# Convolution, silu and splits of the mLSTM branch moved from the heads into the input projection

## The chip, the core and the metric

The kernel runs on one core of a Trainium2 chip. The metric is the device time of one execution in microseconds (us); lower is better. The kernel before takes 4286.54 us (median of three executions, 4284.75 to 4287.95). Engines are named as the profile does: PE (matmuls), PEld (its weight loads), DVE, ACT, POOL, SP. Each has a queue of its own, and they meet at semaphores.

## The reference, cut to what matters

One transformer-like block on 512 tokens of width 2048: a norm, an input projection, an S5 branch with a gated linear unit (GLU), an mLSTM branch, a merge, an output projection, and a PEER layer with 16384 experts. The part that the change touches is the front of the mLSTM branch:

```python
def causal_conv(x, w, b):
    seq = x.shape[1]
    xp = jnp.pad(x, ((0, 0), (CONV_WIDTH - 1, 0), (0, 0)))
    out = b
    for j in range(CONV_WIDTH):
        out = out + xp[:, j:j + seq] * w[j]
    return out
...
    xc = jax.nn.silu(causal_conv(xm, conv_w, conv_b))
    q = jnp.einsum('bshd,hde->bshe', heads(xc), w_q).astype(f32)
    k = (jnp.einsum('bshd,hde->bshe', heads(xc), w_k) * MLSTM_HEAD_DIM ** -0.5).astype(f32)
    v = jnp.einsum('bshd,hde->bshe', heads(xm), w_v).astype(f32)
...
    h = h * mh_gain.astype(f32) + skip.astype(f32) * xc.astype(f32)
```

xm is 1536 channels wide: four heads of 384 channels, each three blocks of 128. q, k and the skip use xc, v uses xm itself.

## The kernel before

**Arithmetic.** Every matmul on weights is done three times on fp32r halves: an operand is split into a high part (a copy that ACT writes, `whi`, `xc_hi`) and a low part (operand minus high part, `wlo`, `xc_lo`, on DVE or POOL), and `mm3` (L1730) runs high x high, high x low, low x high. Activations lie transposed, 128 channels on the partitions and 512 tokens along a row.

**Weights.** All weights come as a stream of units of 128x2048 (1 MB). SP loads a unit into one of two `raw` buffers when its last content has been split (L301 to L306). ACT makes `whi` (L653), DVE `wlo` (L1038), each one unit ahead of PE. In the input projection one unit gives one output block of 128 channels: 16 x 3 matmuls, 10.9 us.

**Input projection.** Blocks 0 to 3 are the S5 input, 4 to 15 xm (U_XM to U_Z), 16 to 27 z, 28 to 59 the merge gates. For each xm block ACT splits the next unit (L690), waits for PE, copies the result from PSUM to `stage[:, k, :]` (L693) and stores it to the DRAM tensor `spill` (L695). Two stage buffers take turns. DVE only makes the low parts of the units (L1204 to L1206). Behind the xm blocks DVE prepares the gates of the mLSTM: two additions (L1211, L1212) and one operation (L1213), whose semaphore `ge_sem` releases ACT's exponential (L702); after it ACT goes on with the z blocks, their first unit split first. POOL is idle in this stage; its first work afterwards is the store of the gates (L370).

**S5 and GLU.** During blocks 28 to 59 the S5 recurrence runs beside the projection. Then come eight GLU units of four output chunks each (PE from L1811): PE makes value and gate chunks into two pairs of banks, ACT takes the sigmoid of a gate chunk (L756), DVE multiplies (L1322, waits for the store of ya two products earlier), POOL multiplies with `sa`, stores `ya_d` (L435) and reloads `sa` (L440). Before this loop POOL loads xmr, the three xm blocks of head 0, from `spill` (L416), and DVE, ACT and POOL make the convolution, silu and split of head 0: `conv(step, 0, c)`, `conv_high(0, c)`, `conv_lo(0, c)`.

**Heads.** Four heads, one after another, in an order written out by hand for each engine. PE in `head` (L1839): six q and k blocks from xc (nine matmuls each), the mean of the previous head's output (L1829, waits for POOL's multiplication with z) after the third, its squares (L1836, wait for ACT's L768, that for DVE's L1330) after the fifth, then scores and values, den (L1877) and the weighted sum. Banks are few: a block's bank is free when DVE has made its low part (L1364, L1366), and scores(0) waits for all six. Into this order the convolution of the *next* head is woven: DVE `conv` (L1294, one L1300 and three L1302 per block, on xmr), ACT `conv_high` (silu into `xcf` L736, copy to `xc_hi` L739) and POOL `conv_lo` (L422), between the blocks q1, q2 and k4 or k5. `xmr` is reloaded for the next head in `next_xm` (L472), which waits until the convolution and the low parts of xm have read it. POOL's `skips` (L459) add `xc_hi` and `xc_lo` back together for the skip term.

## Time and profile before

| | us |
|---|---|
| median of three executions | 4286.54 |
| the profiled execution, its own time | 4285.1 |
| its span from first to last instruction | 4283.6 |
| busy: PE, DVE, ACT, POOL | 4065.0, 2508.7, 1226.7, 1129.3 |
| xm and part of the z blocks of the projection | 107 to 334 |
| GLU | 827 to 927 |
| heads and their tail | 927 to 1195 |
| everything behind (merge, output projection, PEER) | 1195 to 4283.6 |

A row of a timeline gives the start, the duration, the engine, the line, the operation, and in brackets how long the engine was idle before and what released it. A row of windows gives a stretch, its length, the busy time of each engine in it with its instructions, the granted clock of PE as a share of full speed (1.00 is 2.4 GHz, 0.50 is 1.2 GHz), the busy share of the DMA engines and GB/s. A matmul of 512 columns is shown as 0.39 us long, and one starts every 0.227 us at full clock.

### The profile page before, as it was taken

The page shows a single profiled execution, that of the slowest core. Times are in us where ns is not written, and L with a number is a line of the kernel's source. Part 1 is how long each engine was busy: PE and PEld are TensorE (multiplying, and loading weights), DVE is VectorE, ACT ScalarE, POOL GpSimd, SP SyncE. Part 2 cuts the span into 40 slices and gives each one's busy share as a digit, 9 for nine tenths or more (in the row PEclk, how much of TensorE's full clock was granted, in tenths as well). Part 3 has the DMA queues.
Part 4 walks back from the last instruction along what each step waited for, and adds up shares of the span by engine and source line. Part 5 has one row for each costly group of instructions (what it writes and reads, how often), then busy time and mean ns, then how long its engine had stood idle before and what let it go on. Part 6 is the DMA issues. An engine that isn't in the chain of part 4 may idle for free.

```text
span 4283.6 us, 54780 instructions
## 1 busy us (share of the span) xinstructions
PE 4065.0 (95%) x19189; PEld 3474.4 (81%) x19189; DVE 2508.7 (59%) x3563; ACT 1226.7 (29%) x1282; POOL 1129.3 (26%) x742
## 2 busy tenths in 40 slices
PE   7999999887789989999999999999989999999997
PEld 4887666665677768888888888888879999999996
DVE  5226888837653254454566666222237888788874
ACT  3232222234322222222233333222222222232222
POOL 1002334433211144545300000000012444444432
PEclk9999999998899989999999999999999999999998
DMA  3332222342154344554677777866767888888883
GB/s 120 120 115 98 98 100 96 108 152 79 51 175 142 127 135 162 173 170 161 209 238 239 255 241 238 295 216 215 222 232 262 302 306 325 308 327 304 307 315 114
DMA packets 225639, 840.57 MB, mean 196 GB/s; under 512 B 21720, under 2 KB 60136, under 8 KB 157600
## 3 DMA queue, kind: packets, MB, share of 16 engines
q1 hardware_dynamic: 96432, 454.07, 29.3%
q10 hardware_dynamic: 95808, 207.64, 15.6%
q0 software_dynamic: 33328, 178.08, 11.5%
q8 instruction: 25, 0.41, 0.0%
q14 instruction: 46, 0.38, 0.0%
HBM read 753.70 MB, written 220.23 MB: 227 GB/s over the span
## 4 chain that ended last, share of the span: by engine, by line
PE 72%; DVE 13%; issue 6%; DMA 4%; ACT 3%; POOL 2%; DVEq 1%; ACTq 0%; SPq 0%; POOLq 0%
PE mm L1732 18%; PE mm L1733 18%; PE mm L1734 17%; DMA raw<-stream 3%; PE pv L1732 3%; PE pv L1733 3%; PE pv L1734 3%; DVE wlo L1038 2%; PE sc L1734 1%; PE sc L1733 1%; PE sc L1732 1%; DVE acc L1658 1%; ACT whi L653 1%; DVE tab L1258 1%; POOL el L611 1%
## 5 line engine op out<-in xcount | busy, mean ns | idle before, releaser
L1038 DVE TENSOR_TENSOR wlo<-raw,whi 128x2048 fp32r<-128x2048 f32 x328 | 753.4, 2297 | 882.4 <-ACT whi L653 881.9
L653 ACT ACTIVATE whi<-raw 128x2048 fp32r<-128x2048 f32 x380 | 727.4, 1914 | 499.6 <-issue 198.7
L1732 PE MATMUL mm<-t_hi,whi 128*128 128x512 f32 x2048 | 798.5, 390 | 0.0
L1733 PE MATMUL mm<-t_lo,whi 128*128 128x512 f32 x2048 | 797.8, 390 | 0.0
L1734 PE MATMUL mm<-t_hi,wlo 128*128 128x512 f32 x2048 | 797.3, 389 | 0.0
L1734 PEld LDWEIGHTS mm<-t_hi,wlo 128*128 128x128 f32 x2048 | 384.6, 188 | 80.4
L1732 PEld LDWEIGHTS mm<-t_hi,whi 128*128 128x128 f32 x2048 | 384.8, 188 | 78.1
L1733 PEld LDWEIGHTS mm<-t_lo,whi 128*128 128x128 f32 x2048 | 384.8, 188 | 77.7
L1732 PE MATMUL mm<-hn_hi,whi 128*128 128x512 f32 x960 | 380.6, 396 | 34.3 <-DVE hn_lo L1074 19.3
L1733 PE MATMUL mm<-hn_lo,whi 128*128 128x512 f32 x960 | 376.6, 392 | 0.0
L1734 PE MATMUL mm<-hn_hi,wlo 128*128 128x512 f32 x960 | 375.9, 392 | 0.0
L617 POOL DMA_INDIRECT gv<-ev_d,idx_v x128 | 230.1, 1798 | 513.7 <-DVE acc L1658 468.7
L550 POOL TENSOR_TENSOR wlo<-raw,whi 128x2048 fp32r<-128x2048 f32 x52 | 239.3, 4603 | 301.0 <-ACT whi L653 301.0
L1658 DVE SCALAR_TENSOR_TENSOR acc<-gv,ac,acc 128x2048 f32<-128x2048 f32 x127 | 298.2, 2348 | 32.5 <-DMA gv<-ev_d,idx_v 30.3
L894 ACT ACTIVATE sgl<-mm 128x512 f32<-128x512 f32 x128 | 76.7, 599 | 744.9 <-PE mm L1734 744.8
L1732 PEld LDWEIGHTS mm<-hn_hi,whi 128*128 128x128 f32 x960 | 181.7, 189 | 95.6 <-issue 33.8
L611 POOL DMA_INDIRECT el<-up_d,idx_e x128 | 198.2, 1548 | 88.0 <-DVE ac L1664 49.2
L1734 PEld LDWEIGHTS mm<-hn_hi,wlo 128*128 128x128 f32 x960 | 181.9, 189 | 38.5
L1733 PEld LDWEIGHTS mm<-hn_lo,whi 128*128 128x128 f32 x960 | 182.0, 190 | 36.5
L961 ACT ACTIVATE actb<-gl 128x384 f32 (+1 forms) x128 | 67.3, 526 | 492.5 <-DVE gl L1633 484.6
L1732 PE MATMUL pv<-actb,whi 128*128 (+1 forms) x512 | 173.0, 338 | 13.7 <-DVE wlo L1038 13.7
L1732 PE MATMUL mm<-actb,whi 128*128 (+1 forms) x512 | 171.7, 335 | 0.4 <-DVE wlo L1038 0.3
(395 smaller groups left out, 7553.1 us busy)
## 6 DMA issues: line engine op xcount, KB each, us to landing
raw<-stream SPq DMA_DIRECT2D x380, 1024.0 KB, 4.9
ev_d<-stream ACTq DMA_DIRECT2D x128, 1024.0 KB, 6.1
up_d<-sgl ACTq DMA_DIRECT2D x128, 256.0 KB, 2.1
g_d<-gst ACTq DMA_DIRECT2D x12, 2048.0 KB, 11.5
gg<-g_d SPq DMA_DIRECT2D x15, 1536.0 KB, 12.0
gl<-up_d SPq DMA_DIRECT2D x120, 192.0 KB, 5.0
spill<-stage ACTq DMA_DIRECT2D x56, 256.0 KB, 2.0
x<-xT SPq DMA_DIRECT2D x4, 1024.0 KB, 9.4
```

The source lines that it names most:

```text
L550: pool.tensor_tensor(wlo[:, nk, :], raw[:, nk, :], whi[:, nk, :].bitcast(F32), ALU.subtract)\
L611: pool.indirect_dma_start(el[:, s:s + 1], None, ups_flat, bass.IndirectOffsetOnAxis(ap=idx_e[:, s:s + 1], axis=0)).then_inc(el_in, 16)
L617: pool.indirect_dma_start(gv[s % 3][:], None, ev_d, bass.IndirectOffsetOnAxis(ap=idx_v[:, 0, s:s + 1], axis=0))\
L653: act.activation(whi[:, k, :], raw[:, k, :], ACT.Copy).then_inc(hi_done, 1)
L894: act.activation(sgl[:, k, :], mm[k][:], ACT.Gelu_apprx_tanh).then_inc(proj_free, 1)
L961: act.activation(actb[:, par, 0, v, :], gl[:, v % 2, :], ACT.Copy).then_inc(acthi_done, 1)
L1038: dve.tensor_tensor(wlo[:, k, :], raw[:, k, :], whi[:, k, :].bitcast(F32), ALU.subtract)\
L1258: ins = dve.scalar_tensor_tensor(ts_[:, w:2 * w], tc_[:, 0:w], psin, dtmp[:, 1, 0:w], ALU.mult, ALU.add)
L1658: dve.scalar_tensor_tensor(acc[:], gv[b][:], ac_cols[:, s, :], acc[:], ALU.mult, ALU.add)\
L1732: pe.matmul(out, lh, rh, start=start, stop=False)
L1733: pe.matmul(out, lh, rl, start=False, stop=False)
L1734: return pe.matmul(out, ll, rh, start=False, stop=stop)
```

## The change

The convolution, the silu and the split into high and low part are done for each of the twelve xm blocks during the input projection. DVE convolves from `stage` into `cv` as soon as ACT has copied the block there. ACT takes the silu in place and makes the high part into `xcs`, one block later in its order: split of the next unit, silu and high part of the block before, copy of the block itself. DVE makes the low part in the following block, after the weights' low part. POOL stores both parts to a new DRAM tensor `xc_d`, 512 KB a block. Before the GLU loop POOL loads them all into `xc_hi` and `xc_lo` with four transfers on its queue (two of 768 KB for head 0, two of 2304 KB for heads 1 to 3), placed behind the loads of xmr and sa. PE waits for them before head 0 and before head 1. The heads no longer hold `conv`, `conv_high`, `conv_lo` and the waits that belonged to them. xmr is still loaded per head, for v. A buffer of its own, `nt_h`, serves the Newton step of `scale`.

```diff
+            with pool.Fori(0, MC // 2) as p:
+                for k in range(2):
+                    pool.wait_ge(xclo_done, 2 * p + k + 1)
+                    pool.dma_start(xc_d[2 * p + k].rearrange("r p t -> p r t"), xcs[:, k, :, :]).then_inc(xc_out[k], 16)
...
-            for c in range(HC):
-                conv_lo(0, c)
-
+            for k in range(2):
+                pool.wait_ge(xc_out[k], 16 * (MC // 2))
+            xc_src = xc_d.rearrange("c r p t -> r p c t")
+            for g, cs in enumerate((slice(0, HC), slice(HC, MC))):
+                for r, dst in enumerate((xc_hi, xc_lo)):
+
+                    pool.wait_ge(proj_done, O_GLU)
+                    pool.dma_start(dst[:, cs, :], xc_src[r, :, cs, :]).then_inc(xc_in[g], 16)
...
-                pool.wait_ge(cv_done, 3 * h + 3)
                 pool.wait_ge(xmlo_done, 3 * h + 3)
                 pool.dma_start(xmr[:], xm_heads[h + 1]).then_inc(xm_in, 16)
...
-                if not last:
-                    for c in range(HC):
-                        conv_lo(h + 1, c)
                 if not first:
-
-                    pool.wait_ge(xclo_done, 3 * h + (3 if last else 6))
                     skips(h - 1, (0, 1))
...
+            def conv_high(n, k):
+
+                act.wait_ge(cv_done, n + 1)
+                act.activation(cv[:, k, :], cv[:, k, :], ACT.Silu).then_inc(silu_done, 1)
+                met()
+                act.wait_ge(silu_done, n + 1)
+                act.wait_ge(xc_out[k], 16 * (n // 2))
+                act.activation(xcs[:, k, 0, :], cv[:, k, :], ACT.Copy).then_inc(xchi_done, 1)
+
+            def mlstm_tile(m, k, first=False):
+                n = 2 * (m - U_XM // 2) + k
+                next_hi(m, k, (proj_done, 2 * m + k))
+                if not first:
+                    conv_high(n - 1, 1 - k)
+                act.wait_ge(proj_done, 2 * m + k + 1)
+                act.wait_ge(stage_out[k], 16 * (m - U_XM // 2))
+                act.activation(stage[:, k, :], mm[k][:], ACT.Copy).then_inc(proj_free, 1)
+                act.wait_ge(proj_free, 2 * m + k + 1)
+                act.dma_start(spill[2 * m + k - U_XM], stage[:, k, :]).then_inc(stage_out[k], 16)
+
+            mlstm_tile(U_XM // 2, 0, first=True)
+            mlstm_tile(U_XM // 2, 1)
+            with act.Fori(U_XM // 2 + 1, U_Z // 2) as m:
+                for k in range(2):
+                    mlstm_tile(m, k)
+            conv_high(MC - 1, 1)
...
-            for c in range(HC):
-                conv_high(0, c)
-
...
                 qkv(0)
                 qkv(1)
-                if not last:
-
-                    if not first:
-                        act.wait_ge(hf_done, 3 * (h - 1))
-                    act.wait_ge(xclo_done, 3 * h + 3)
-                    conv_high(h + 1, 0)
                 qkv(2)
-                if not last:
-                    conv_high(h + 1, 1)
                 if not first:
                     tail_squares(h - 1)
                 qkv(3)
                 qkv(4)
                 qkv(5)
-                if not last:
-                    conv_high(h + 1, 2)
...
+            def conv(n, k):
+
+
+                one, count = stepper(ml_step, 3 * n)
+                o, i = cv[:, k, :], stage[:, k, :]
+                tap = [cols(V_CW + MC * j, MC)[:, n, :] for j in range(4)]
+                dve.wait_ge(proj_free, U_XM + n + 1)
...
+            next_lo(U_XM // 2, 0)
+            conv(0, 0)
+            next_lo(U_XM // 2, 1)
+            conv_lo(0, 0)
+            conv(1, 1)
+            with dve.Fori(U_XM // 2 + 1, U_Z // 2) as m:
                 for k in range(2):
                     next_lo(m, k)
+                    conv_lo(2 * m + k - U_XM - 1, 1 - k)
+                    conv(2 * m + k - U_XM, k)
+            conv_lo(MC - 1, 1)
...
-            dve.wait_ge(xm_in, 16)
-            for c in range(HC):
-                conv(step, 0, c)
-
...
-                dve.wait_ge(silu_done, MC if last else 3 * h + 6)
-                newton(one, rs[:], rd[:], cv[:, 1, :])
+                newton(one, rs[:], rd[:], nt_h[:])
...
-                pe.wait_ge(xclo_done, 3 * h + 3)
...
             pe.wait_ge(onesr_done, 1)
+            pe.wait_ge(xc_in[0], 32)
             head(0, True)
+            pe.wait_ge(xc_in[1], 32)
             with pe.Fori(1, HEADS) as h:
```

## Rows read from the trace of the kernel before

**Rows 1.** Windows: projection, GLU, heads; start:end, length, busy time of PE, PEld, DVE, ACT, POOL

```profile
107.00:334.00 227.00, 227.00 (x1003) 188.00 (x1003) 54.98 (x33) 62.73 (x51) 0.00 (x0) 1.00 0.34 120
827.00:927.00 100.00, 92.80 (x388) 75.90 (x389) 40.75 (x37) 35.93 (x37) 41.36 (x48) 0.93 0.49 172
927.00:1195.00 268.00, 188.14 (x798) 147.59 (x796) 172.87 (x245) 101.67 (x157) 79.82 (x72) 0.85 0.22 70
```

**Rows 2.** Waits of PE from 820 to 1200: total us, times, longest us

```profile
PE st L1829 <- POOL hh L452: 20.3, 3, 9.6
```

**Rows 3.** Timeline of PE in the GLU and the heads, rows behind a gap

```profile
846.35 0.80 PE L1732 MATMUL mm<-y_hi,whi 128*128 128x512 f32 x1 [4.85 <-DVE vt L1322]
...
956.13 0.79 PE L1732 MATMUL sc<-q_hi,k_hi 128*128 128x512 f32 x1 [17.42 <-DVE k_lo L1366]
...
998.96 3.78 PE L1836 MATMUL dn<-ex,ones 128*128 128x512 f32 x4 [5.03 <-ACT ex L768]
...
1016.11 0.39 PE L1732 MATMUL sc<-q_hi,k_hi 128*128 128x256 f32 x1 [1.34 <-DVE pf L1383]
...
1060.55 2.46 PE L1836 MATMUL dn<-ex,ones 128*128 128x512 f32 x4 [3.89 <-ACT ex L768]
...
1118.37 1.88 PE L1836 MATMUL dn<-ex,ones 128*128 128x512 f32 x4
...
1124.58 0.50 PE L1732 MATMUL sc<-q_hi,k_hi 128*128 128x512 f32 x1 [1.41 <-DVE k_lo L1366]
```

**Rows 4.** Windows, for the granted clock behind the busy times (third from the end)

```profile
848.00:853.00 5.00, 5.00 (x18) 3.99 (x18) 2.01 (x1) 0.00 (x0) 3.74 (x5) 0.77 0.59 192
...
942.00:959.00 17.00, 2.87 (x7) 2.30 (x8) 9.61 (x16) 9.12 (x14) 3.80 (x3) 0.51 0.11 46
...
997.00:1004.00 7.00, 5.04 (x7) 2.19 (x7) 4.95 (x8) 3.74 (x7) 1.27 (x1) 0.51 0.00 1
...
1062.00:1065.00 3.00, 3.00 (x6) 1.35 (x5) 2.65 (x5) 0.50 (x2) 0.00 (x0) 0.50 0.00 0
```

**Rows 5.** Timelines of ACT before the first sigmoid, of DVE in head 0

```profile
842.86 0.63 ACT L739 ACTIVATE xc_hi<-xcf 128x512 fp32r<-128x512 f32 x1
...
939.83 0.55 DVE L1300 TENSOR_SCALAR cv<-xmr,vec 128x512 f32<-128x512 f32 x1 [7.92 <-DMA xmr<-spill]
...
955.39 0.68 DVE L1366 SCALAR_TENSOR_TENSOR k_lo<-mm,k_hi 128x512 fp32r<-128x512 f32 x1
```

**Rows 6.** Timelines: one block's convolution, silu and split; a unit's low part

```profile
944.10 0.63 ACT L736 ACTIVATE xcf<-cv 128x512 f32<-128x512 f32 x1
944.82 0.63 ACT L739 ACTIVATE xc_hi<-xcf 128x512 fp32r<-128x512 f32 x1
...
993.70 0.54 DVE L1300 TENSOR_SCALAR cv<-xmr,vec 128x512 f32<-128x512 f32 x1
994.38 2.54 DVE L1302 SCALAR_TENSOR_TENSOR cv<-xmr,vec,cv 128x511 f32<-128x511 f32 x3
...
240.94 2.29 DVE L1038 TENSOR_TENSOR wlo<-raw,whi 128x2048 fp32r<-128x2048 f32 x1 [8.22 <-ACT whi L653]
```

**Rows 7.** Timeline of ACT between the xm blocks and the z blocks

```profile
235.77 0.60 ACT L693 ACTIVATE stage<-mm 128x512 f32<-128x512 f32 x1 [7.51 <-PE mm L1734]
...
237.70 1.28 ACT L653 ACT_TABLE_LOAD   x1
238.99 1.92 ACT L653 ACTIVATE whi<-raw 128x2048 fp32r<-128x2048 f32 x1
246.72 1.28 ACT L693 ACT_TABLE_LOAD   x1 [5.81 <-PE mm L1734]
```

**Rows 8.** DMA issues (KB each, median us to landing); landings of xres, min/median/max

```profile
h<-h_d POOLq DMA_DIRECT2D x1, 4096.0 KB, 15.1
...
key_raw<-keys POOLq DMA_DIRECT2D x1, 1024.0 KB, 7.2
...
DMA to landing us min/median/max: 2.8/3.0/9.6
```

More of the change, by code:

```diff
@@ L456, in skips @@
                 for c in blocks:
-                    if c >= 2:
-                        pool.wait_ge(hf_done, 3 * h + c - 1)
+                    pool.wait_ge(hf_done, 3 * h + c - 1 if c >= 2 else 3 * h)
                     pool.tensor_tensor(xcf[:, c % 2, :], xc_hi[:, 3 * h + c, :].bitcast(F32),
@@ L1291, in _ @@
                 assert count[0] == S5_STEPS, count
-            def conv(one, h, c):
-                dve.wait_ge(silu_done, 3 * h + 1 if c == 2 else 3 * h)
-                o, i = cv[:, c % 2, :], xmr[:, c, :]
-                tap = [cols(V_CW + MC * j, MC)[:, 3 * h + c, :] for j in range(4)]
-                one(dve.tensor_scalar(o, i, tap[3], cols(V_CB, MC)[:, 3 * h + c, :], ALU.mult, ALU.add))
-                for lag in (1, 2, 3):
-                    ins = dve.scalar_tensor_tensor(o[:, lag:T], i[:, 0:T - lag], tap[3 - lag], o[:, lag:T],
-                                                   ALU.mult, ALU.add)
-                    if lag < 3:
-                        one(ins)
-                    else:
-                        ins.then_inc(cv_done, 1)
             split_lo(U_GLU // 2, 1)
-            dve.wait_ge(xm_in, 16)
-            for c in range(HC):
-                conv(step, 0, c)
             with dve.Fori(0, 4) as q:
@@ L1392, in head @@
                 qkv(1)
-                if not last:
-                    dve.wait_ge(xm_in, 16 * h + 32)
-                    conv(one, h + 1, 0)
                 qkv(2)
-                if not last:
-                    conv(one, h + 1, 1)
                 if not first:
@@ L1402, in head @@
                 qkv(4)
-                if not last:
-                    conv(one, h + 1, 2)
                 if not first:
@@ L1443, in _ @@
                 dve.wait_ge(ya_out[b], 16 * 8)
-            one, count = stepper(ml_step, 0)
+            one, count = stepper(ml_step, 3 * MC)
             head(one, 0, True, False)
```

40 lines of the change are left out of this document (21 added, 19 removed).

## The prediction

> **What bounds the kernel now.** I read the busy shares of each stage first, then what PE waits for, then the timelines of PE, DVE and ACT at those waits. In the stretch in which the input projection makes the mLSTM blocks PE is busy 227.00 of 227 us, while DVE has 55 and ACT 63 [rows 1]: whatever DVE and ACT do there beside it is free as long as every next weight block is split before PE asks for it. In the gated linear unit (GLU) PE has 92.8 of 100 us. In the four heads and their tail it has 188 of 268 us: 80 us without a matmul, the only place here with something to win. The reader is to see in [rows 3] which waits make them up. Before the scores of head 0 PE is idle for 17.42 us, before the squares (L1836) 5.03 us in head 1 and 3.89 in head 2, before the third score block 1.34 us, and inside the GLU 4.85 us. The longest waits besides, 20.3 us in three pieces, stand before the mean over the channels [rows 2]; a reciprocal and the finish of the previous head lead there, and no convolution. The clock follows the gaps: it stands at 0.51 of full, that is at its lower level of 1.2 GHz, from 942 to 959 and from 997 to 1004, at 0.50 from 1062 to 1065, and at 0.77 in the five microseconds behind the GLU's gap [rows 4].
>
> **Which of these waits are the convolution's.** Head 0: PE has all six q and k blocks by 938.7 (17.42 before 956.13). But DVE starts its next convolution only when the reload of xmr has landed (939.83, 7.92 us idle), and its last k_lo, which releases the scores, starts at 955.39, behind three convolutions that alternate with ACT's silu [rows 5]. Heads 1 and 2: ACT stands at silu and its split ahead of the squares. Head 3 has no convolution and is the template: its squares start without a wait, the first four take 1.88 us where they took 3.78 in head 1 and 2.46 in head 2, it has no wait before its third score block, and it keeps only the 1.41 us between the last k block and the scores [rows 3]. GLU: ACT is in the third split of head 0 until 843.5, so the first sigmoids are late [rows 5].
>
> **Heads, part by part.** Removed from DVE per block: 0.54 + 2.54 us; from ACT 0.63 + 0.63; from POOL one subtraction [rows 6]. None of that sum is the gain; the gaps are.
> Head 0: 17.42 becomes 1.41, that is 16.0. What is late next is the load of the gate rows, which follows xmr on POOL's queue; it delays the first exponents by some 3 us, but PE has two score and two value blocks (about 6.8 us) before it needs them, so I take nothing for it. The scores also ran at half clock from 956.13 to about 959.5, 3.4 us for 1.7 us of work [rows 3, 4]. Together 17.7.
> Head 1: 5.03 and 1.34 go. From the start of the squares at 998.96 until about 1004 PE works at half clock, 5.0 us for 2.5 us of work [rows 4], so 2.5 more. Together 8.9.
> Head 2: 3.89, the same 1.34, and three microseconds at half clock (1062 to 1065) for 1.5 of work. Together 6.7.
> The waits before the mean stay: their chain starts at the last value block of PE itself, and is the same in all heads. The xm reload loses a wait on the convolution and is issued no later. POOL's two skip additions now stand directly behind the gate loads, as in head 3.
> Heads: 33.3 us gained.
>
> **GLU.** The 4.85 us go, and with them some 2 us that the following matmuls lost at low clock (0.77 over five us, [rows 4]); 6.8. Against it: 6 MB (24 blocks of 256 KB) of loads are put on POOL's queue ahead of the reload of sa and of the stores of ya, and DVE's third product waits for the first of these stores. How the queue treats this a row shows: the reloads of xres land in 3.0 us in the median, but in up to 9.6 us where they stand behind the 1 MB of key_raw, which itself took 7.2; so the later ones wait for the earlier. The 4 MB of h came in 15.1 us beside other traffic [rows 8], so 6 MB take about 22.6; issued from about 828 on, they end near 851. PE needs the third product at about 852 (two units of four chunks, 48 matmuls at 0.227 us each, behind 841.5). So it is level to within a microsecond. I take 1 us of stall; bounds 0 (queue not in order) and 8 (loads a third slower, or behind a weight load, with the clock lost again). GLU: 5.8 gained, bounds 6.8 gained and 1 lost.
> The Trainium skill, page "DMA: Bandwidth & Descriptors", section "Queues, rings and completion order", says the same of order (descriptors are consumed in ring order, rows take turns), and its section "Bandwidth" puts the HBM side at about 358 GB/s for a core: by that figure alone an estimate for the 6 MB is 17.6 us, the stall would be nothing and the time 1 us lower.
>
> **Input projection.** Added per block, twelve times: convolution 3.2, low part 0.69 on DVE; silu and high part 1.35 on ACT; a 512 KB store on POOL's queue, where nothing else stands until the gates. DVE then has 2.29 + 3.2 + 0.7 = 6.2 us and ACT 1.92 + 0.60 + 1.35 = 3.9 of the 10.9 us that a block takes PE [rows 6, 7]. The order within a block: stage at 0.2 to 0.8, convolution until 4.0, low part of the next weights until 6.3, and PE wants it at 10.9. The cover is 4.6 us. Here, 0, until the stage ends.
> At its end the cover is missing. The last mLSTM block is copied at 235.77. Until now ACT went on with the gates' exponential at once, loaded a table (1.28) and had the next weights split at 240.9, DVE by 243.2; PE asks for them at about 246.5, when it leaves the block between [rows 7]. After the change ACT's exponential waits for DVE's three gate operations, which stand behind the last convolution and its low part, and that one waits for ACT. The chain: 236.4, convolution 3.0, silu and split 1.4, low part 0.75, three gate operations at about 0.75 each (a third of the 2.54 that three of 511 columns take is 0.85, [rows 6]), exponential 0.65, table 1.3, high part 1.95, low part 2.3: 250.0. PE waits 3.5 us (at 3.2 for the convolution 3.7). A second table load on the chain (silu and exp) would make it 4.8, and a gap of this size cost clock above; I put 5 us, bounds 2 and 8.
> The trace shows one load as 1.28 us with the next activation right behind it (237.70 + 1.28 = 238.98) [rows 7]. The Trainium skill, page "ScalarE: Activation LUTs", section "What ACT_TABLE_LOAD costs", adds a drain of 1.38 us to each; this row shows none. By the page the seam would cost 1.4 us more for each load on its chain.
>
> **The sum.** The profiled execution took 4285.1 us (span 4283.6), 1.4 below the median of 4286.54. Heads -33.3, GLU -5.8, seam +5: -34.1. 4251.0 for that execution, 4252.4 for a median: 4252.
>
> **The rivals.**
> A, forecast: about 4252, within 8 us (bounds of seam and GLU, and clock windows that fall differently). 0.60.
> B, queue: the loads of xc on POOL's queue end at 860 or later, PE stands 8 us in the GLU and starts again at half clock. For it: the order shown in [rows 8], and 2 KB pieces where h had long ones. Against it: the rate above. 4252 + 8 to 10 = 4261. 0.14.
> C, only head 0: the gaps in heads 1 and 2 change owner, since DVE or the mean's chain is late there anyway. For it: DVE is busy 173 of 268 us in this stretch [rows 1]. Against it: head 3. Gain without 15.5: 4268. 0.09.
> D, better: no stall in GLU, seam 2 us, less time at low clock in the heads: 4244 or lower. 0.09.
> E, slower: the projection's cover fails. Per block DVE's low part now stands behind the convolution, that behind ACT's stage, and ACT's silu behind both. If this circle takes longer than PE's 10.9 us, each of twelve blocks pays the excess. It stands at 6.3, so it decides from 4.6 us more per block than worked out, and the whole is slower by over 0.2% from 3.6 us beyond that (43 us over twelve blocks eat the 34). What could add as much is a table load before each of a block's four activations: at 1.28 us they make 11.4 us, an excess of 0.5, 6 us in all, 4258; at double that price 16.5 us, an excess of 5.6, 67 us in all, 4319. Against it: the one load in [rows 7] is followed at once by its activation, ACT is idle 7.51 us before a stage, and DVE is busy a quarter of this stretch. 0.04.
> The double price is near that of the Trainium skill, page "ScalarE: Activation LUTs", section "What ACT_TABLE_LOAD costs": about 2.66 us for a switch; its section on table sets lists copy among the functions of every set, and by that E can't come about.
> F, the edit moves little: the heads' waits turn out to be others' and the seam and the queue cost what B and their upper bounds say; within 8.6 us of now. 0.04.
>
> **Chances and range.** 0.2% is 8.6 us, about what a measurement of this kernel can tell from no change. Faster: A to D nearly whole, 0.91; same: F and a corner of C, 0.05; slower: E, 0.04. The range reaches from the better half of D to B and the near edge of C: 4240 to 4267.
>
> **What would show it.** PE in the projection without a gap up to about 246, then one gap of 3 to 5 us behind which ACT's whi ends near 248. In the GLU no gap at the third unit, or one that a late landing of ya ends. Head 0: one gap of 1.4 before its scores in place of 17.4, and first scores near 940 on the old clock. Heads 1 and 2: no gap before the squares, none before the third score block; the gaps of 9.6 and 8.0 before the mean still there. What would make me wrong: a gap in every projection block (E), a GLU gap over 5 us (B), or squares that still wait (C).

## The result and the profile after

The changed kernel takes 4250.6 us (median of 4 runs, 4247.31 to 4252.15) against 4286.13 us for the kernel before on the same chip (4 runs, 4284.75 to 4287.95). The ratio is 0.9917, with a 95% interval of 0.9904 to 0.9930. Run a second time, in a longer comparison, it took 4251.5 us, ratio 0.9926 (0.9912 to 0.9939). The forecast was 4252.

The page of the profiled execution of the changed kernel, which took 4247.31 us itself: its span, the engines, the queue that GpSimd issues on (packets, MB, share of 16 DMA engines), and the shares of the chain that ended last.

```profile
span 4245.8 us, 54861 instructions
...
PE 4051.5 (95%) x19189; PEld 3466.7 (82%) x19189; DVE 2514.0 (59%) x3575; ACT 1226.3 (29%) x1280; POOL 1132.2 (27%) x746
...
q0 software_dynamic: 39728, 190.67, 12.5%
...
PE 76%; DVE 10%; issue 5%; DMA 3%; POOL 2%; ACT 2%; DVEq 0%; ACTq 0%; SPq 0%; POOLq 0%
```

The busy time of no engine fell by anything like 35 us; PE's 13.5 us less are the same 19189 matmuls, of which fewer run at the lower clock. DVE and ACT do the same work as before, at another place. What fell is waiting: PE's share of the chain rose from 72 to 76%, DVE's fell from 13 to 10.

Windows of the changed kernel that answer to [rows 1]; each stage starts elsewhere now, so the second and third are set to its start. Columns: start:end, length, busy time of PE, PEld, DVE, ACT and POOL, granted clock, DMA share, GB/s.

```profile
107.00:334.00 227.00, 223.31 (x979) 184.41 (x978) 93.51 (x97) 80.10 (x76) 8.70 (x12) 0.99 0.42 143
...
836.00:928.00 92.00, 90.44 (x385) 74.20 (x386) 30.56 (x24) 30.10 (x29) 39.80 (x48) 0.97 0.74 252
...
927.00:1195.00 268.00, 212.35 (x935) 169.78 (x936) 166.92 (x226) 99.31 (x144) 73.50 (x71) 0.90 0.29 94
```

The projection: DVE went from 55 to 93.5 us and ACT from 63 to 80, and PE lost 3.7 us, at one place. The GLU is whole in 92 us, where it needed 98.4, though its DMA share went from 0.49 to 0.74. In the same 268 us behind it PE is busy 212 us instead of 188 and its clock is 0.90 instead of 0.85.

The timeline of PE after, rows at the places of [rows 3]. Columns: start, duration, engine, line, operation, and in brackets the idle time before it and who ended it.

```profile
251.33 0.65 PE L1738 MATMUL mm<-hn_hi,whi 128*128 128x512 f32 x1 [3.69 <-DVE wlo L1043]
...
835.84 0.79 PE L1738 MATMUL mm<-y_hi,whi 128*128 128x512 f32 x1 [3.52 <-DVE y_lo L1323]
...
927.74 0.47 PE L1738 MATMUL mm<-xc_hi,whi 128*128 128x512 f32 x1 [1.56 <-DVE vt L1337]
...
941.65 0.50 PE L1738 MATMUL sc<-q_hi,k_hi 128*128 128x512 f32 x1 [1.41 <-DVE k_lo L1379]
...
977.74 1.88 PE L1842 MATMUL dn<-ex,ones 128*128 128x512 f32 x4
...
1022.55 1.22 PE L1835 MATMUL st<-hh,ones 128*128 128x512 f32 x1 [9.62 <-POOL hh L462]
...
1076.04 1.22 PE L1835 MATMUL st<-hh,ones 128*128 128x512 f32 x1 [8.15 <-POOL hh L462]
...
1282.22 0.70 PE L1738 MATMUL mm<-mg_hi,whi 128*128 128x512 f32 x1 [3.42 <-DVE mg_lo L1474]
```

Between 835.84 and 927.74 no row of PE has a wait in brackets: the GLU's gap is gone. Head 0 has 1.41 us before its scores for 17.42. The four squares of head 1 (977.74) have no wait and take 1.88 us, the value of head 3 before. The waits of 9.6 and 8.2 us before the means (1022.55, 1076.04) stand as they stood. New is the first row, 3.69 us where the projection goes over from the mLSTM blocks to the z blocks.

The two fixed points by which I measure the heads with their tail are the first q matmul and the first matmul of the output projection. In the kernel before they are these rows of PE's timeline:

```profile
926.20 0.47 PE L1732 MATMUL mm<-xc_hi,whi 128*128 128x512 f32 x1 [1.56 <-DVE vt L1322]
...
1316.63 0.49 PE L1732 MATMUL mm<-mg_hi,whi 128*128 128x512 f32 x1 [3.39 <-DVE mg_lo L1468]
```

So the stretch is 390.4 us before and 1282.22 - 927.74 = 354.5 after, 35.9 less. Summed over PE's rows, its gaps of over half a microsecond in this stretch went from 81.6 to 54.8 us; the other 9 us are matmuls that no longer ran at half clock. The two executions differ by 4285.1 - 4247.3 = 37.8 us: 35.9 here, 6.5 in the GLU (98.4 to 91.9), 3.4 behind the output projection's start, where the code is the same, less 8.1 by which the GLU starts later (827.78 to 835.84). The 3.4 don't belong to the change: in a second profiled execution of the changed kernel (4250.89 us) that part is 0.1 us longer than before, and the other three terms are the same within 0.2. The whole gain is made in the heads; GLU and seam nearly cancel.

### The profile page after: what moved, and what is told of

The parts are those of the page before. It is cut to its first block, busy times and chain, and to the rows that moved or that the text cites. A ratio compares the mean times of both kernels' runs of the same rounds, so it can differ in the third digit from the quotient of the medians.

```text
span 4245.8 us, 54861 instructions
## 1 busy us (share of the span) xinstructions
PE 4051.5 (95%) x19189; PEld 3466.7 (82%) x19189; DVE 2514.0 (59%) x3575; ACT 1226.3 (29%) x1280; POOL 1132.2 (27%) x746
## 3 DMA queue, kind: packets, MB, share of 16 engines
q1 hardware_dynamic: 96432, 454.07, 29.4%
## 4 chain that ended last, share of the span: by engine, by line
PE 76%; DVE 10%; issue 5%; DMA 3%; POOL 2%; ACT 2%; DVEq 0%; ACTq 0%; SPq 0%; POOLq 0%
PE mm L1738 18%; PE mm L1739 18%; PE mm L1740 18%; PE pv L1738 3%; PE pv L1740 3%; PE pv L1739 3%; DMA raw<-stream 2%; DVE wlo L1043 2%; PE sc L1740 2%; PE sc L1739 2%; PE sc L1738 2%; POOL el L615 1%; ACT whi L657 1%; DVE acc L1664 1%; PE st L1740 1%
## 5 line engine op out<-in xcount | busy, mean ns | idle before, releaser
L1738 PE MATMUL pv<-actb,whi 128*128 (+1 forms) x512 | 172.8, 337 | 12.0 <-DVE wlo L1043 11.9
L1739 PE MATMUL pv<-actb,whi 128*128 (+1 forms) x512 | 171.9, 336 | 0.0
```

Source lines behind the costliest of these rows:

```text
L1738: pe.matmul(out, lh, rh, start=start, stop=False)
L1739: pe.matmul(out, lh, rl, start=False, stop=False)
```

## The experiments

**The changed kernel again, and the gates' three operations moved.** The theory for the seam is a serial chain that ends with the next block's low part; its length in steps is known, so each step that leaves it must shorten the gap by its own time.

> The changed kernel itself, on the chip and in the rounds of the three that follow: every theory gives about 4251 us, 35 below the kernel before. PE gap of 3.7 us at 251 us, none in the GLU.

It took 4251.5 us (4250.69 to 4252.87). The gap at the seam is 3.69 us again, the GLU has none, the scores of head 0 wait 1.41 us. The first kernel of the seam's own moves the first three gate operations ahead of the first convolution:

```diff
             next_lo(U_XM // 2, 0)
...
+            ts(gi, pv[0][0:HEADS, :], vec[0:HEADS, V_BI:V_BI + 1], None, ALU.add)
+            ts(gf, pv[0][32:32 + HEADS, :], vec[32:32 + HEADS, V_BF:V_BF + 1], None, ALU.add)
+            dve.scalar_tensor_tensor(g1, gf, -1.0, gf, ALU.mult, ALU.max).then_inc(ge_sem, 1)
             conv(0, 0)
...
             conv_lo(MC - 1, 1)
...
-            ts(gi, pv[0][0:HEADS, :], vec[0:HEADS, V_BI:V_BI + 1], None, ALU.add)
-            ts(gf, pv[0][32:32 + HEADS, :], vec[32:32 + HEADS, V_BF:V_BF + 1], None, ALU.add)
-            dve.scalar_tensor_tensor(g1, gf, -1.0, gf, ALU.mult, ALU.max).then_inc(ge_sem, 1)
```

> The three gate operations on DVE move from behind the last convolution to the front of the mLSTM blocks; nothing else. Theory (the seam is one chain over ACT and DVE, each link counts): gates and the last low part (2.9 us) leave the chain, but ACT's exponential now follows its table load (1.28), which was hidden behind the wait. The exponential starts at 243.5 instead of 245.1, PE's gap at 251 falls from 3.7 to 2.1 us; 1.6 us less, and up to 1.7 more if the clock doesn't fall behind a gap of 2 us: 4248 to 4249. Rival (ACT's table loads alone set the seam): gap stays at 3.4 or more, 4251.

It took 4248.95 us (4247.78 to 4255.01), ratio 0.9922 (0.9908 to 0.9935). The same row of its PE timeline:

```profile
249.42 0.50 PE L1738 MATMUL mm<-hn_hi,whi 128*128 128x512 f32 x1 [2.11 <-DVE wlo L1043]
```

3.69 went to 2.11 with the three gate operations off the chain. The GLU starts 3.3 us earlier (832.59 against 835.85 in the run beside it): 1.6 from the gap, the rest because the clock no longer falls behind it (0.57 of full from 251 to 255 in the run beside it). The gap is the evidence; by their times alone (4251.5 against 4248.95, with ranges that overlap) the two kernels can't be told apart.

**The seam taken away.** Here the gates stand early too, and both halves of the first z block's weights (unit 16) are split before the last convolution's silu and low part.

```diff
                     mlstm_tile(m, k)
+            next_hi(U_Z // 2, 0, (proj_done, U_Z))
             conv_high(MC - 1, 1)
...
+            next_lo(U_Z // 2, 0)
             conv_lo(MC - 1, 1)
+            next_lo(U_Z // 2, 1)
```

> As e1_gates_early, and ACT splits the next weights before the last silu, DVE makes their low part before the last block's low part. Theory: the new chain was the only cost in the projection, so PE's gap at 251 (3.7 us) and the 3.4 us at half clock behind it (1.7) are gone, and the clock windows of the S5 stage fall as before: 5.4 to 7 us less, 4244 to 4245. Rival (the cost moves: silu and low parts are late for the next block or its stores): a gap of 2 us or more at the next block, 4248 or above.

It took 4246.47 us (4243.04 to 4254.22), ratio 0.9915 (0.9902 to 0.9929), where 4244 to 4245 was expected, and 4245.5 us (4244.79 to 4252.88) when run again; of this second run:

> e2_seam once more, beside the run of both repairs on the same chip: 4246 to 4248 by either theory, with a GLU gap of 0 to 3 us that depends on where ya_d lands behind the loads.

No row of PE near 250 has a wait in brackets in either. The GLU starts at 828.70, 7.15 us earlier than in the run of the changed kernel beside it. But head 0 starts only 4.4 us earlier (923.51 against 927.88). What took 2.8 back is a row of PE's timeline in the GLU, here of the two runs in order:

```profile
856.36 0.50 PE L1744 MATMUL mm<-y_hi,whi 128*128 128x512 f32 x1 [3.04 <-DVE vt L1343]
```

```profile
856.85 0.79 PE L1744 MATMUL mm<-y_hi,whi 128*128 128x512 f32 x1 [4.19 <-DVE vt L1343]
```

In the second the clock stood at 0.51 from 856 to 863, and the GLU took 97.5 us where the changed kernel's takes 91.9. The margin at the GLU's third product, level to a microsecond in the forecast, is that thin: in the nine profiled executions whose GLU and queue are the changed kernel's (those told of so far and later ones) this gap was 0 (twice), 0.66, 1.19, 2.67, 3.03 (twice), 3.04 and 4.19 us. The mean is 2.0 us.

**What this wait is: the order in POOL's queue.** First the rows of the changed kernel: POOL's issues of the loads of xc and of the first store of ya_d (timeline of POOL), and the landing times of all its stores.

```profile
834.48 0.77 POOL L437 DMA_DIRECT2D xc_hi<-xc_d  x1
835.22 0.79 POOL L437 DMA_DIRECT2D xc_lo<-xc_d  x1
835.98 1.03 POOL L437 DMA_DIRECT2D xc_hi<-xc_d  x1
836.99 1.02 POOL L437 DMA_DIRECT2D xc_lo<-xc_d  x1
...
849.55 0.62 POOL L445 DMA_DIRECT2D ya_d<-vt  x1 [0.71 <-POOL vt L443]
```

```profile
DMA to landing us min/median/max: 2.3/2.4/10.2
```

The last load takes 22.1 us, so it lands at 859.1, 23 us behind the start of the GLU. The first ya_d store, issued at 849.55, takes 10.2 us and lands at 859.8, 0.7 behind the loads; its fellows take 2.4. The test: 2 MB more behind the loads, data that nothing uses, in the same queue.

```diff
                     pool.dma_start(dst[:, cs, :], xc_src[r, :, cs, :]).then_inc(xc_in[g], 16)
+            pool.dma_start(extra[:], xc_src[1, :, 0:8, :]).then_inc(extra_in, 16)
```

> Behind the four loads of xc POOL loads 2 MB more on the same queue, into a place that nobody reads; ACT waits for it before head 0, when it has long landed. Theory (queue in order; PE would ask for the third product about 1 us after it is there): the stores of ya land 6 to 7 us later (866), PE gets a gap of 5 to 6 us at the third GLU unit and a stretch of half clock behind it: 6 to 8 us slower than the changed kernel, 4257 to 4259. Rival (the stores share the queue and don't wait behind the loads): no gap, 4251.

It took 4259.67 us (4255.49 to 4260.55), ratio 0.9941 (0.9925 to 0.9958). Its row of PE and its ya_d landings:

```profile
867.94 0.80 PE L1742 MATMUL mm<-y_hi,whi 128*128 128x512 f32 x1 [8.08 <-DVE vt L1341]
```

```profile
DMA to landing us min/median/max: 2.3/2.4/18.5
```

The extra load lands at 866.43, the store right behind it at 867.10. The mechanism holds; my size was too small: the gap is 8.1 us instead of 5 to 6, and the GLU is 9.4 us longer than the changed kernel's. The counter-test puts the four loads on ACT's queue, declared as plain float:

```diff
-                    pool.dma_start(dst[:, cs, :], xc_src[r, :, cs, :]).then_inc(xc_in[g], 16)
+                    act.dma_start(dst[:, cs, :].bitcast(F32), xc_src[r, :, cs, :].bitcast(F32)).then_inc(xc_in[g], 16)
```

> The four loads of xc are issued by ACT on its own queue at the start of the GLU, as plain float32, instead of by POOL. Theory (the order within POOL's queue alone makes DVE wait): the first store of ya lands in 2.5 to 5 us instead of 10.2, DVE's wait of 4.9 us goes, PE is unchanged: 4251. Rival (the DMA engines are full, whoever issues): the store takes 8 us or more here too.

It took 4249.83 us (4248.84 to 4250.77), ratio 0.9921 (0.9904 to 0.9937). Its ya_d landings:

```profile
DMA to landing us min/median/max: 2.3/2.4/6.3
```

Now the last load is the one that waits, 26.9 us, and lands at 863.8, while the first store lands at 854.55. The 5.6 us of this store are a little above the 2.5 to 5 expected. No gap, GLU 91.6 us. It gains little over the changed kernel by itself, since that had little or no gap to lose; in the two profiled executions with the loads on this queue (this one and that of both repairs, below) the GLU has no gap, which is too few to say that it never comes. The Trainium skill, page "DMA: Bandwidth & Descriptors", section "Queues, rings and completion order", says that descriptors are consumed in ring order on each DMA engine, for the queues of SP and ACT; these runs show the small store behind the bulk loads also on the queue that GpSimd issues on, of which that passage doesn't speak.

**Are the short packets to blame?** The loads of xc, declared float32r at both ends, travel in packets of 2048 bytes; plain float ones have 4096.

```diff
-                    pool.dma_start(dst[:, cs, :], xc_src[r, :, cs, :]).then_inc(xc_in[g], 16)
+                    pool.dma_start(dst[:, cs, :].bitcast(F32), xc_src[r, :, cs, :].bitcast(F32)).then_inc(xc_in[g], 16)
```

> The four loads of xc declared as plain float32 on both sides, same bytes, same queue. In the changed kernel they move as 2 KB packets of 114 ns, 28 us in all, and the third product of DVE stands 4.9 us before the store of ya behind them lands; PE is not held (it asks about 1 us later). Theory (queue in order, level with PE by a microsecond): packets of 4 KB at 159 ns as for xmr, the last load lands some 7 to 9 us earlier (852 instead of 859), DVE's wait is gone, PE's times in the GLU are the same: 0 us, 4251. Rival (PE is slowed by the loads elsewhere in the GLU, by weights that come late): 1 to 3 us faster.

A miss. It took 4251.59 us (4250.80 to 4253.15), as the changed kernel. The DMA view of both for 843 to 857 (all traffic, then GpSimd's queue: packets, MB, share), first the plain loads, then the changed kernel:

```profile
DMA packets 1258, 5.53 MB, mean 395 GB/s; under 512 B 40, under 2 KB 40, under 8 KB 1129
...
q0 software_dynamic: 1113, 4.46, 83.2%
```

```profile
DMA packets 2352, 5.55 MB, mean 396 GB/s; under 512 B 35, under 2 KB 35, under 8 KB 2223
...
q0 software_dynamic: 2207, 4.48, 112.3%
```

Half the packets, the same bytes in the same time: the last load lands after 22.10 us instead of 22.12. The windows view gives the DMA engines' share in this stretch as 1.02 and 1.32: they are busy throughout with either, and packets of half the size lose nothing. My price for the packets was an inference from their mean durations, and it was wrong.

**The reload of xmr.** In the kernel before, DVE's first convolution in head 0 waited 7.92 us for the reload of xmr. How much of the 17.42 is this wait alone? One wait is put back in, with no work behind it:

```diff
                 qkv(0)
                 qkv(1)
+                if not last:
+                    dve.wait_ge(xm_in, 16 * h + 32)
                 qkv(2)
```

> In the changed kernel's heads 0 to 2 DVE waits for the reload of xmr before its third low part, as the convolution did; no convolution is made. Theory: in head 0 the low parts stand until the reload lands some 13.6 us into the head, the scores start about 2.6 us later than now (gap 4.0 instead of 1.4), perhaps with 1 to 2 us of low clock; heads 1 and 2 unchanged: 3 to 5 us slower, 4254 to 4256. Rival (the wait for the reload is what made the 17.4 us): gap above 10 us in head 0, 10 us or more slower.

It took 4254.44 us (4254.31 to 4256.81), ratio 0.9934 (0.9918 to 0.9951). Head 0's row of PE:

```profile
945.87 0.50 PE L1740 MATMUL sc<-q_hi,k_hi 128*128 128x512 f32 x1 [3.60 <-DVE k_lo L1379]
```

3.60 us against 1.41: the reload alone is worth 2.2 us of gap, only in head 0. The other 13.8 of the 17.42 needed the work as well. The time is inside the expected 4254 to 4256, but it isn't the wait alone: this execution also has a gap of 3.03 us in its GLU. The stretch from the first q matmul to the output projection is 3.4 us longer than the changed kernel's (357.85 against 354.4).

How far can such a stretch be read? Nine profiled executions of this case have the changed kernel's heads (its own two, and those of the kernels for the seam, the queue, the packets and both repairs together). Their stretches go from 353.7 to 358.5 us, while their gaps of over half a microsecond sum to 54.0 to 54.9 in each; what differs is how long PE runs at half clock. So a difference in gaps is good to about 1 us, one between two stretches only to about 5, and the 3.4 can't be put down to the wait.

**The work, engine by engine.** Three kernels put the old work back into heads 0 to 2 at its old places. It is computed a second time into a spare tile and thrown away; projection, stores and loads stay as changed; in the two kernels with DVE's part the reload of xmr waits for the convolutions that read it, as before. First DVE's four steps per block with the reload's wait, and no silu:

```diff
                 qkv(1)
+                if not last:
+                    dve.wait_ge(xm_in, 16 * h + 32)
+                    again(one, h + 1, 0)
                 qkv(2)
+                if not last:
+                    again(one, h + 1, 1)
...
                 qkv(4)
+                if not last:
+                    again(one, h + 1, 2)
```

> The changed kernel with DVE's convolutions of heads 1 to 3 made once more inside the heads at their old places, with their wait for xmr, into a buffer nobody reads; no silu on ACT, nothing on POOL. It does this work twice. Theory: DVE's part alone gives head 0 a gap of 11 to 14 us (of 17.4; the rest was the hand-over to ACT and back), and heads 1 and 2 gaps of 2 to 3 us before the squares (of 5.0 and 3.9): 16 to 22 us slower, about 4270. Rival (the hand-over to ACT's silu is the main cause): gap in head 0 under 8 us, squares without a wait, at most 10 us slower.

It took 4279.02 us (4273.24 to 4283.21), ratio 0.9988 (0.9978 to 0.9997). Its PE rows:

```profile
955.30 0.80 PE L1760 MATMUL sc<-q_hi,k_hi 128*128 128x512 f32 x1 [12.83 <-DVE k_lo L1394]
...
999.46 3.78 PE L1864 MATMUL dn<-ex,ones 128*128 128x512 f32 x4 [5.72 <-ACT ex L787]
...
1059.51 3.48 PE L1864 MATMUL dn<-ex,ones 128*128 128x512 f32 x4 [2.98 <-ACT ex L787]
```

Head 0's gap is inside the expectation and head 2's squares too; head 1's, 5.72, is above it, and so is the time, 27.5 us over the changed kernel's instead of 16 to 22. The traced execution is the slowest of the ten (4283.21 us). The gaps in the stretch are 20.0 us more than in the changed kernel (74.8 against 54.8) and the stretch 27.3 us longer (381.8); the 7 between are matmuls at half clock. Part of the miss is that some of DVE's steps are slower than they were in the kernel before. Head 1 of this kernel, rows of ACT, DVE and POOL, and then the last two of these DVE steps in the kernel before:

```profile
998.77 1.23 ACT L787 ACTIVATE ex<-hh 128x512 f32<-128x512 f32 x2 [11.08 <-DVE hh L1349]
...
988.36 1.76 DVE L1381 SCALAR_TENSOR_TENSOR dz<-xmr,vec,dz 128x511 f32<-128x511 f32 x1 [0.17 <-DVE dz L1379]
990.27 3.79 DVE L1381 SCALAR_TENSOR_TENSOR dz<-xmr,vec,dz 128x510 f32<-128x510 f32 x2 [0.16 <-DVE dz L1381]
...
989.74 0.75 POOL L498 DMA_DIRECT2D sz<-spill  x1
990.50 3.00 POOL L471 TENSOR_TENSOR xcf<-xc_hi,xc_lo 128x512 f32<-128x512 f32 x2
```

```profile
989.45 1.65 DVE L1302 SCALAR_TENSOR_TENSOR cv<-xmr,vec,cv 128x510 f32<-128x510 f32 x2 [0.15 <-DVE cv L1302]
```

Two steps take 3.79 us beside POOL's skip additions (L471) and 1.65 without them; in the kernel before these additions stood behind POOL's low parts, later. With the step ahead of them (1.76 against 0.75) that is 3.1 us in head 1, and in head 2 the three steps take 5.44 us against 3.31. So about 5 of the 27 us are slower steps, and some 22 are DVE's old part, the upper end of what I expected. The additions explain these steps only in part: the step of 1.76 us is over at 990.1, before the first addition starts, and POOL only issues DMAs beside it, as it did in the kernel before beside the step of 0.75. What slows it isn't shown.

The first row corrects a sentence of my prediction: with no silu on ACT at all the squares still wait, since ACT has been idle for 11.08 us until DVE's hh (L1349) comes, which stands behind two convolutions.

Then ACT's part alone, on a constant:

```diff
+            def again(h, c, fresh=False):
+                if not fresh:
+                    act.wait_ge(dz_done, 6 * h + 2 * c)
+                act.activation(dz[:], ones[:, 0:1].to_broadcast([P, T]), ACT.Silu).then_inc(dz_done, 1)
+                met()
+                act.wait_ge(dz_done, 6 * h + 2 * c + 1)
+                act.activation(dz[:], dz[:], ACT.Copy).then_inc(dz_done, 1)
```

> The changed kernel with ScalarE's part of the old hand-over put back alone: in heads 0 to 2 ScalarE runs one silu of a 128x512 tile and one copy of it at each of the three places where it had the convolution's silu and high half before, on a constant, with no work added on VectorE. The result of the kernel is not changed by it. Theory (the heads' gain is mostly VectorE's chain of four steps per tile, with the hand-over between the engines on top; ScalarE's own time is cheap): the gap ahead of head 0's scores stays near 1.4 us, the squares' gaps stay at 0 or reach 1, and the gap of 1.3 us ahead of the third block of scores comes back in some heads: 2 to 5 us slower than the changed kernel, about 4255. Rival (ScalarE's six operations a head and the two engines' waiting for each other are the larger part): 10 us slower or more, 4261 and up, with gaps of 3 us or more ahead of squares or scores that end on ScalarE.

It took 4251.73 us (4249.25 to 4252.23), ratio 0.9927 (0.9912 to 0.9942). Head 0 keeps 1.41 us, no squares wait, and a gap comes back at the third score block of heads 1 and 2 (1.09 and 1.10 us), this one in head 1:

```profile
990.15 0.39 PE L1754 MATMUL sc<-q_hi,k_hi 128*128 128x256 f32 x1 [1.09 <-DVE pf L1412]
```

The stretch is 356.45 us, 2.0 longer than the changed kernel's, and its gaps are 2.2 us more; in the time, where I had expected 2 to 5 us, it can't be told from it. So DVE's part makes some 22 us of the 36 and ACT's 2; the rest had two possible owners: the handing over between DVE and ACT, or POOL's low parts, which the scores waited for. The third kernel has DVE's and ACT's part, each waiting for the other as in the kernel before, in two buffers, and nothing on POOL:

```diff
+                if c == 2:
+                    dve.wait_ge(dsl_done, 6 * h + 2)
+                elif not fresh:
+                    dve.wait_ge(dsl_done, 6 * h)
...
+            def again(h, c):
+                act.wait_ge(dz_done, 3 * h + c + 1)
+                act.activation(dz[:, c % 2, :], dz[:, c % 2, :], ACT.Silu).then_inc(dsl_done, 1)
```

> The changed kernel with the whole old hand-over in the heads put back: VectorE runs the convolution of each block of the next head, in two buffers, ScalarE's silu and copy wait for it, and VectorE's third convolution waits for both; the same places, buffers and waits as before the change, only without GpSimd's low parts. The work is done a second time and its result is thrown away. So far VectorE's part alone made the stretch from the first q product to the output projection 27.4 us longer (381.8 against 354.4), ScalarE's alone 2.0, and the kernel before 36.0. Theory (the rest of about 6.6 us is the handing over between the two engines): the gap ahead of head 0's scores is 16 to 17.5 us, with ScalarE waiting for conv results in between, the squares' gaps 4 to 6, the third score block's 1.1 to 1.4 in two heads, the stretch 387 to 391 us, and the time 4283 to 4287. Rival (the rest belongs to GpSimd's low parts, which the scores had to wait for): head 0's gap stays near 13, the stretch is 381 to 385 us, and the time is 4278 to 4281.

It took 4290.54 us (4287.85 to 4292.88), ratio 1.0016 (1.0006 to 1.0025): all of the gain is gone, and 7 us more. Its PE rows of heads 0, 1 and 2:

```profile
958.44 0.80 PE L1779 MATMUL sc<-q_hi,k_hi 128*128 128x512 f32 x1 [15.70 <-DVE k_lo L1413]
...
1005.19 3.62 PE L1883 MATMUL dn<-ex,ones 128*128 128x512 f32 x4 [7.85 <-ACT ex L786]
...
1067.57 2.93 PE L1883 MATMUL dn<-ex,ones 128*128 128x512 f32 x3 [6.03 <-ACT ex L786]
```

And the timeline of its DVE in head 0:

```profile
944.06 2.32 DVE L1398 SCALAR_TENSOR_TENSOR dz<-xmr,vec,dz 128x511 f32<-128x511 f32 x3
948.28 0.69 DVE L1411 TENSOR_TENSOR q_lo<-sc,q_hi 128x512 fp32r<-128x512 f32 x1 [1.90 <-ACT q_hi L813]
948.89 0.54 DVE L1396 TENSOR_SCALAR dz<-xmr,vec 128x512 f32<-128x512 f32 x1
949.46 2.32 DVE L1398 SCALAR_TENSOR_TENSOR dz<-xmr,vec,dz 128x511 f32<-128x511 f32 x3
953.69 0.69 DVE L1413 SCALAR_TENSOR_TENSOR k_lo<-sc,k_hi 128x512 fp32r<-128x512 f32 x1 [1.90 <-ACT k_hi L813]
```

After each convolution DVE stands 1.90 us: it wants the high half of the next q or k block, and ACT makes that only after the silu and copy of the convolution just finished, for which it had itself stood idle. That alternation is the handing over; the two engines' costs don't overlap, they add. The stretch is 392.55 us, 38.1 more than the changed kernel's, where the parts alone make 29.4: 8.7 us for the handing over. The squares' gaps are 2.8 and 2.1 us above the 5.03 and 3.89 of [rows 3], about what DVE's slower steps make again (3.1 and 2.1 us). That this kernel is slower than the one before has more than this cause: by the traces its stretch is 2.1 us longer (392.55 against 390.43) and its GLU 4.0 us shorter, but the GLU starts 8.0 us later, which is mostly the seam. Head 0, where the steps take 0.75 us as before, has 15.70 us against 17.42. At most these 1.7 us, and what clock hangs on them, are left for POOL's low parts.

The sum for the kernel before is then about 22 us for DVE's part, 2 for ACT's, 9 for the handing over and 3 not told apart. These are stretches of one execution each, the clock in them, and good only to some 5 us. By gaps alone it is firmer: DVE's part brings 20.0 us back, ACT's 2.2 and both with the handing over 30.3, so the handing over is 8.1; without the 5 us of slower steps that leaves about 15, 2 and 8 of the 26.8 us of gaps that the change took away. My expectation for this kernel's stretch (387 to 391) and time (4283 to 4287) was too low, at least in part by these slower steps.

**Both repairs together.** The seam as above and the loads on ACT's queue.

> Both repairs together: the seam of the projection as in e2_seam (high and low halves of unit 16 split ahead of the last convolution, first gate steps ahead of it too), and the four loads of the conv output issued from ScalarE's queue as in e4_act_queue. Theory (e2_seam's 7.2 us of gain at the seam were partly given back in the GLU because ya_d stood behind the loads in one queue; in a queue of its own it can't): no gap of the TensorE at the seam, none in the GLU, GLU about 91.6 us long, heads' start about 920.4 against 927.8, so 5.5 to 7 us faster than the changed kernel, about 4244. Rival (the GLU gives the time back by something else, as the transfers' own rate): the GLU again 93 us or longer with a gap ahead of its third or fourth product, 4246 to 4248, as e2_seam.

It took 4242.07 us (4240.34 to 4246.06), ratio 0.9907 (0.9892 to 0.9922), beside 4245.5 for the seam's repair alone on the same chip. Windows of it, seam and GLU with the columns as above, and the second seam-only run's GLU below:

```profile
236.00:248.00 12.00, 12.00 (x55) 9.93 (x54) 5.60 (x6) 7.58 (x8) 0.72 (x1) 1.00 0.57 196
828.00:920.00 92.00, 90.01 (x385) 74.07 (x386) 31.40 (x25) 30.28 (x29) 35.83 (x45) 0.97 0.69 255
```

```profile
829.00:927.00 98.00, 91.97 (x385) 75.21 (x386) 30.49 (x24) 30.40 (x29) 38.54 (x48) 0.95 0.70 238
```

PE doesn't wait at the seam, the GLU takes 91.5 us with no gap, and head 0 starts at 919.89, where 920.4 was expected and the changed kernel has 927.74. This is the fastest version of the case. It and the changed kernel were timed against the kernel before, not against each other, and the intervals of their ratios (0.9907 here, 0.9917 and 0.9926 there) overlap; the 7.9 us are what the traces show, the medians say 8.5 to 9.4. That is more than the 5.5 to 7 expected. Over the seam's repair alone the medians give 3.4 us, with ranges that overlap (4240.34 to 4246.06, 4244.79 to 4252.88).

## Why the prediction was right

The time fell within 2 us of the forecast, and rival A is what happened. Step by step, by differences between the same rows of both traces:

- **Head 0**, predicted 17.7. From the first q matmul to the scores 29.9 us became 13.9: 16.0, as computed from the gap. From there to the mean 31.0 became 29.4 (scores no longer at half clock): 1.6. Together 17.6. That the late gate rows would cost nothing held: behind the scores PE has no wait until its usual 2.32 us at 957.
- **Head 1**, predicted 8.9: from mean to mean 60.7 us became 51.5, 9.2.
- **Head 2**, predicted 6.7: 62.4 became 53.5, 8.9. This is the term that was too small. Its gaps went as said (3.89 and 1.34); the clock gave 3.7 us instead of the 1.5 that I took from one window. Before, the half-clock stretches between the two means made 18.0 us, in five pieces, after 12.6; I had counted one of them, three microseconds long. Outside the wait before the mean, where half clock costs nothing, they are about 14 and 7 us.
- **The waits before the mean** stayed, 9.62 and 8.15 us for 9.61 and 8.04. Head 3 and the tail, where nothing was predicted, changed by +1.0 and -1.3.
- **Heads in all**: 33.3 predicted, 35.9 found. The prediction had 27.6 of gaps and 5.7 of clock; found were 26.8 and 9.1.
- **GLU**, predicted 5.8: 6.5. The loads end 23.3 us behind the GLU's start; 23 was worked out. The stall of 1 us that I took didn't come in this execution; over nine of them it is 0 to 4.2 us, 2 in the mean, so the term was somewhat small, for the reason named. Rival B's mechanism, a store behind the loads in one queue, is real (the kernel with 2 MB more); it lost on the rate alone. Its "2 KB pieces" argument fell with the plain loads.
- **Seam**, predicted 5: the gap is 3.69 us, the sum said 3.5 to 3.7. The GLU starts 8.1 us later than before. Of this 1.0 was there before the first mLSTM block (among the executions of kernels with the changed projection this start varies by 1.7), 5.6 is the seam, the gap and the half clock behind it, and about 1.4 is clock that falls elsewhere (half clock from 359 to 366 before, from 364 to 374 after). The chain itself, on ACT in the changed kernel:

```profile
240.85 0.63 ACT L704 ACTIVATE cv<-cv 128x512 f32<-128x512 f32 x1 [3.45 <-DVE cv L1218]
...
242.21 1.28 ACT L729 ACT_TABLE_LOAD   x1
245.10 0.63 ACT L729 ACTIVATE gt<-gt 4x512 f32<-4x512 f32 x1 [1.60 <-DVE gt L1247]
245.74 1.28 ACT L657 ACT_TABLE_LOAD   x1
247.04 1.91 ACT L657 ACTIVATE whi<-raw 128x2048 fp32r<-128x2048 f32 x1
```

The chain was to end at 250.0 on the clock of before; the last copy now stands 1.03 us later, and whi ends at 248.95 and the low part at 251.27. The second table load that I feared is there (242.21), but hidden: ACT waits 1.60 us more for the gates behind it. The load on the chain starts at 245.74, where the activation before it ends at 245.73; it ends at 247.02, and the next activation starts at 247.04. The Trainium skill, page "ScalarE: Activation LUTs", section "What ACT_TABLE_LOAD costs", counts 1.38 us of drain with every switch; here there is none, neither ahead of the load nor behind it.

- **The projection's cover** held: one gap, at the end, none in the twelve blocks. Rival E's condition didn't come: DVE was at 41% in this stretch, with room.
- **Rivals C and F** are refuted by the rows at 941.65 and 977.74 and by head 2's 8.9 us: all three heads gained.

That the forecast fits within 2 us is in part luck. Against the second profiled execution of the changed kernel, whose part behind the heads is as before, the terms are off by 2.6 us (heads) and 0.6 (GLU) one way and by 3.1 (the GLU's later start, 8.1 instead of 5) the other, and nearly cancel. In the first one they leave 3.7, most of it the 3.4 us in code that the change doesn't touch.

What the prediction had wrong in the mechanism is a reason. It said of heads 1 and 2 that ACT stands at silu and split ahead of the squares, and that the gaps come from there. ACT's work alone brings back none of the squares' gaps; DVE's alone brings back both. The kernel with DVE's part put back is nearly one that moved only ACT's and POOL's share away, and it gained 5 us (ratio 0.9988).

Open is why the same GLU has a gap of 3 to 4 us in some executions and none in others. It goes with the time that the last load of xc takes: 22.0 to 22.3 us in the four executions with 0 to 1.2 us of gap, 23.2 to 23.6 in the four with 2.7 to 3.0, and 24.9 in the one with 4.2. That speaks for the queue's rate and against PE as what sets it, but no run varied the rate alone. What makes it vary (the weight blocks that are fetched beside it may come at another moment in each) wasn't tried. That half clock follows gaps is seen in each trace; why one gap moves it more than another isn't explained here.

## What to carry to other kernels

Where PE waits for single results, work that two other engines do by turns costs the sum of both plus the handing over, and its place in the busy shares is small: the same convolutions cost 36 us in the heads (27 of gaps, of which about 15 by one engine, 2 by the other and 8 by waiting for each other, and 9 of clock) and, with 4.6 us of cover per block by the sum, nothing in the projection. Price the move's two ends: what was done "in the next stage anyway" now ends a chain at the seam (5.6 us), and a bulk load put into a queue delays whatever small store comes next in that queue (0 to 8 us); both can be taken away by order alone, here for another 8 us. And to a gap add what the clock does behind it: here 9 us on 27 of gaps.

## What the runs showed of the hardware

- Packets of 2048 and of 4096 bytes moved 5.55 and 5.53 MB in the same 14 us, at 396 and 395 GB/s, reads and writes together; a mean duration of a packet (114 and 167 ns by the shares above) says little about the rate once all DMA engines are busy.
- With the bulk on another queue than the small stores, both are served: a 256 KB store took 5.6 us beside 6 MB of loads, against 10.2 us behind them and 2.4 alone, and the last load then took 26.9 us instead of 22.1.
- Two steps of DVE on 128x510 floats took 3.79 us beside GpSimd's additions of 128x512 floats and 1.65 without them. A step just ahead of the additions took 1.76 us instead of 0.75 as well, for a reason that no run shows.
- A gap can cost more than itself: 1.6 us less at 250 moved the GLU's start by 3.3 us. 5.0 less (3.7 there, and 1.3 at the gates' gap near 362 to 369, 6.83 to 5.54) moved it by 7.2. And executions of the same code differ by up to 5 us in the heads with the same gaps, by the clock alone.
